# A conditioned decoder layer on one core: the first two modulations, with half of the row tiles of w_ada multiplied on TensorE

## The chip, the cores and the metric

One NeuronCore of a Trainium2 chip runs the whole layer in one launch. The metric is the device time of that launch in microseconds (us), as the median of several runs. A lower time is better. TensorE is called PE here (PEld is its weight load), VectorE DVE, ScalarE ACT, GpSimd POOL, and SyncE SP, which issues the transfers.

## What is computed

The reference is one layer of a decoder with adaptive normalization. What matters here is its beginning, for x of 1024 tokens by 1024 features and one condition vector c of 1024:

```python
c_act = jax.nn.silu(c)
mod = c_act @ w_ada[l] + b_ada[l]            # w_ada: 1024 x 9216
sh1, sc1, ga1, sh2, sc2, ga2, sh3, sc3, ga3 = jnp.split(mod, 9, axis=-1)
h = modulate(rms_norm(x, g_ffn1[l]), sh1, sc1)       # h * (1 + scale) + shift
x = x + 0.5 * ga1[:, None, :] * swiglu(h, w_gate1[l], w_up1[l], w_down1[l])
```

Then follow a mixer with two attention groups, a second SwiGLU with sh3, sc3 and ga3, and a last norm. The change touches sh1 and sc1, the first two of the nine modulations, and the squares of x for the first norm.

## The kernel before

x is held feature by feature: 8 tiles (NT) of 128 features by 1024 tokens in f_main. Large products are made of pairs of float32r operands, a high part (a cast, on ACT) and a low part (the rest, a subtraction on DVE for x and on POOL for weights), in three matmuls each; each engine runs its own program in order, and semaphores join them. The order is written out by hand.

The opening, up to the first product, goes so:

- SP (L741 to L750) issues x in four transfers of 1 MB, row tile 0 of the first gate and up weights (`pair_row`, 0.5 MB each), w_ada for the shift (j = 0) and the scale (j = 1) in four transfers of 1 MB each, two row tiles of 128 rows in each, and row tile 1 of gate and up.
- ACT squares the eight x tiles (L1491) into x_sq, splits two weights (`weight_high`, L1031), takes the root of the mean square of each half of the tokens (`std`, L997), copies DVE's sums out of PSUM (`ada_copy`, L1163), splits the other six weights of the first pair, and then goes in turns through `shifted` (L1008, x times nrm_a plus shift) and `x_high` (L1020, the cast).
- PE multiplies ones by each square tile (L2527, 8 tiles by two halves), then `mod_mm` (L2520) turns each of DVE's two sums into a modulation: 8 matmuls with a 128x128 float32 weight and a column of ones. The products of the first SwiGLU follow (`piece`, L2536 to L2538).
- DVE sums, for one modulation after the other, c_act times w_ada over the eight row tiles (`ada_start`: L1926 for the first, L1929 for the others) into PSUM, with the two reciprocals (L1831) between; then adds the bias (`mod`, L1934), makes nrm_a = (1 + scale) times gain (`shift_scale`, L1837), and the low parts of x (`x_low`, L1844).
- POOL splits off the low parts of the first two weights (`weight_low`, L1635), multiplies the first eight chunks of x by the reciprocal (`scaled_x`, L1630), does the other six weights and the other eight chunks.

A chunk is 128 features by 512 tokens; there are 16 of x. The first pair of weights has eight blocks (g = 0 to 7, PRELUDE), four of row tile 0 and four of row tile 1. PE goes through the first half of the tokens in two parts of four steps: a step multiplies one chunk with four blocks, twelve matmuls of 512 columns. Blocks 0 to 3 serve the first part, 4 to 7 the second. When POOL has done blocks 6 and 7, SP issues the next pair's loads (L650).

The other seven modulations are summed by DVE later, inside the first SwiGLU, and turned by the same `mod_mm`. The semaphore s_ada_used counts DVE's tiles, s_mod_mm PE's modulations, s_mods the finished ones.

Of the kernel before, what the change touches and what calls it, by code (L numbers as in the profile page):

```python
# [21 lines left out]
ALU = mybir.AluOpType  # L22
# [3 lines left out]
P = 128  # L26
D = 1024
T = 1024
NT = D // P
HALF = 512  # L30
NH = T // HALF
# [3 lines left out]
N_MOD = 9  # L35
# [125 lines left out]
GATE, UP = 0, 1  # L161
# [44 lines left out]
W_SUM_AT = {e: k + 1 for k, e in enumerate(W_SUM_ORDER)}  # L206
MOD_STEPS = [(j, part) for j in range(N_MOD) for part in ((0, 1) if j in (GA1, GA3) else (0,))]
MOD_AT = {e: k + 1 for k, e in enumerate(MOD_STEPS)}


# [66 lines left out]
def build(nc, aps, outs):  # L277
    ctx = ExitStack()
    with ctx:
# [3 lines left out]
        def sem(name):  # L283
            return ctx.enter_context(nc.semaphore(name))
# [75 lines left out]
        ps_mod0, ps_mod1 = ps[:, 4, 0:NT], ps[:, 5, 0:NT]  # L360
        ADA0 = 2 * NT
        ps_stat = ps[:, 6:8, :].rearrange("p a b -> p (a b)")
# [96 lines left out]
        s_ada = [sem(f"ada_in{r}") for r in range(8)]  # L459
        s_ada_used = sem("ada_used")  # L460
        s_mod_mm = sem("mod_mm")
        s_mods = sem("mods_done")
# [180 lines left out]
        def _(sp):  # L643
# [8 lines left out]
            def pair_row(f, b, row):  # L652
                sp.dma_start(pair_raw[b][:, row], w_pair[f][b][row]).then_inc(fsem[f][("row0", "raw")[row]][b], 16)
# [86 lines left out]
            for i in range(4):  # L740
                sp.dma_start(x[:, 2 * i:2 * i + 2, :], aps["xT"][2 * i:2 * i + 2].rearrange("n p t -> p n t")).then_inc(s_x[i], 16)  # L741
            for b in (GATE, UP):
                pair_row(0, b, 0)
            for j in range(2):
                for i in range(4):
                    sp.dma_start(ada_first[:, 16 * j + 2 * i:16 * j + 2 * i + 2, :],
                                 aps["w_ada"][2 * i * P:(2 * i + 2) * P, j * D:(j + 1) * D].rearrange("(r p) c -> p r c", p=P)).then_inc(s_ada[4 * j + i], 16)
            for b in (GATE, UP):
                pair_row(0, b, 1)
            gate_up_loads(0, 0)  # L750
# [226 lines left out]
        def _(act):  # L977
# [180 lines left out]

            def ada_copy(j):

                act.wait_ge(s_ada_used, NT * (j + 1))
                for h in range(NH):
                    act.copy(ada_sum[j][:, halves(h)], ada_acc[j][:, halves(h)]).then_inc(s_ada_sb, 1)  # L1163

            def x_added(base, s):
# [323 lines left out]
            for n in range(NT):  # L1489
                act.wait_ge(s_x[n // 2], 16)  # L1490
                act.activation(x_sq[n], x[:, n, :], ACT.Square).then_inc(nsem["sq"], 1)  # L1491
            for g in range(2):
                weight_high(0, g)
            std(0, 0)
            std(0, 1)
            ada_copy(0)
            ada_copy(1)
            for g in range(2, PRELUDE):
                weight_high(0, g)
            shifted(0, 0)  # L1500
            for i in range(4):
                shifted(0, i + 1)
                x_high(0, 1, i)
            first_pair(0, 0)
            gate_up(0)
# [85 lines left out]
        def _(pool):  # L1591
# [221 lines left out]
        def _(dve):  # L1813
# [96 lines left out]
            def ada(p, m):  # L1910

                dve.wait_ge(s_ada[m % 4], 16 * (1 + 2 * (p - 2) + m // 4 + 1))
                if m == 0:
                    if p > 2:
                        dve.wait_ge(s_ada_sb, 4 + p - 2)
                    dve.tensor_scalar(ps_stat, ada_raw[0], c_act[:, 0:1], None, ALU.mult).then_inc(s_ada_used, 1)
                else:
                    dve.wait_ge(s_ada_used, ADA0 + 8 * (p - 2) + m)
                    dve.scalar_tensor_tensor(ps_stat, ada_raw[m % 4], c_act[:, m:m + 1], ps_stat, ALU.mult, ALU.add).then_inc(s_ada_used, 1)

            def ada_start(j, m):

                acc, w = ada_acc[j], ada_first[:, 16 * j + m, :]
                dve.wait_ge(s_ada[4 * j + m // 2], 16)
                if m == 0:
                    dve.tensor_scalar(acc, w, c_act[:, 0:1], None, ALU.mult).then_inc(s_ada_used, 1)  # L1926
                else:
                    dve.wait_ge(s_ada_used, NT * j + m)
                    dve.scalar_tensor_tensor(acc, w, c_act[:, m:m + 1], acc, ALU.mult, ALU.add).then_inc(s_ada_used, 1)  # L1929

# [142 lines left out]
            dve.wait_ge(s_c, 1)  # L2073
            for m in range(4):
                ada_start(0, m)
            reciprocal(0, 0)
            for m in range(4, 6):
                ada_start(0, m)
            reciprocal(0, 1)
            for m in range(6, NT):  # L2080
                ada_start(0, m)
            for m in range(NT):
                ada_start(1, m)
# [417 lines left out]
        def _(pe):  # L2501
# [13 lines left out]

            def mod_mm(out, total, ready=None):
                for m in range(NT):
                    if ready is not None and m % 4 == 0:
                        pe.wait_ge(s_ada_sb, ready + m // 4 + 1)
# [4 lines left out]
            for n in range(NT):  # L2524
                pe.wait_ge(nsem["sq"], n + 1)
                for h in range(NH):
                    mm = pe.matmul(stat_of[0][h], ones_f[:], x_sq[n][:, halves(h)], start=n == 0, stop=n == NT - 1)  # L2527
                    if n == NT - 1:
                        mm.then_inc(nsem["mm"], 1)
            mod_mm(ps_mod0, ada_sum[0], 0)  # L2530
            mod_mm(ps_mod1, ada_sum[1], 2)
            pe.wait_ge(nsem["std"], 2)

# [24 lines left out]
            def gate_up(f, k):  # L2558
# [26 lines left out]
                for g in range(PRELUDE, N_PROD):  # L2585
# [10 lines left out]
                    if f == 0 and 2 <= p <= 8 and (b, q) == (UP, 4):  # L2596
                        pe.wait_ge(s_ada_sb, 4 + p - 1)
                        pe.wait_ge(s["sil"], z["sil"] + 4 * p + 3)
                        mod_mm(ps_mod, ada_sb)

            def down(f, norm):
# [3 lines left out]
                for e in DOWN:  # L2605
# [9 lines left out]
                    if t == 0:  # L2615
                        if n == 0 and f == 0:
                            pe.wait_ge(s_ada_sb, 4 + N_MOD - 2)
                        if n >= 2:
                            pe.wait_ge(s["sil" if n < 5 else "act"], z["sil" if n < 5 else "act"] + 4 * (PAIRS - 1) + (0, 0, 1, 4, 3, 1, 3, 4)[n])
# [361 lines left out]
```

## Time and profile before

| | |
|---|---|
| median of 3 runs | 2453.43 us (2452.48 to 2454.91) |
| profiled execution | 2450.02 us, of which the span is 2448.1 us |
| PE busy | 2316.3 us, 95% of the span |
| DVE, POOL, ACT busy | 1385.6, 1249.8, 1088.6 us |
| transfers | 314.98 MB, 129 GB/s in the mean |
| PE's first product | 58.47 us after the span's start |

The span runs from the first to the last instruction; the profiled execution is one run with its own time, and the rows further down are from it. In a timeline a row is: start, length (of several instructions in a row, from the first start to the last end), engine, line, operation, output<-input, shapes, count, and in brackets the idle time before it with what ended it. "issue" is time in which the engine waited for nothing that the profile shows. Matmul records are one or two per instruction: a float32 matmul leaves two.

### The profile page before, as it was taken

Reading aid. Unit: us, or ns where it says so; the run is one execution under the profiler, and the core shown is the slowest. Engines: PE = TensorE matmul, PEld = TensorE weight load, DVE = VectorE, ACT = ScalarE, POOL = GpSimd, SP = SyncE. Lnnn points to the kernel's source line nnn. Section 1 sums busy time; section 2 is a strip of 40 time slices with the busy share of each in tenths; the row PEclk is TensorE's granted clock in tenths of the full one; section 3 lists DMA queues with packets and bytes.
Section 4 is the critical chain, followed back from the end, with each engine's and each line's share of the span. In section 5 each row is a group of like instructions: output and inputs, shape, how many; then the busy total and the mean of one; then the engine's idle time right before and its main releaser. Section 6 shows DMA issues by size and latency. Waiting matters only on the chain. (4 is left out here: it accounts for less than half of the span.)

```text
span 2448.1 us, 30080 instructions
## 1 busy us (share of the span) xinstructions
PE 2316.3 (95%) x10920; PEld 1884.8 (77%) x10920; DVE 1385.6 (57%) x1664; ACT 1088.6 (44%) x2060; POOL 1249.8 (51%) x967
## 2 busy tenths in 40 slices
PE   4999999999999899999799999999789999999997
PEld 2788888888877777788677877777578888888885
DVE  5846555266557755742588888575463323225554
ACT  4533333323445443333688888423543333323332
POOL 3454444445564555444557545355745555435473
PEclk7999999999999999999899999999999999999998
DMA  6155544265451433343803046323212222245362
GB/s 254 59 185 176 189 174 160 75 227 168 151 168 48 142 120 128 143 170 129 248 14 88 18 110 173 105 93 130 94 53 85 83 82 94 73 169 175 116 188 88
DMA packets 128946, 314.98 MB, mean 129 GB/s; under 512 B 13408, under 2 KB 34016, under 8 KB 128800
## 3 DMA queue, kind: packets, MB, share of 16 engines
q1 hardware_dynamic: 127824, 310.76, 38.5%
q10 hardware_dynamic: 976, 2.29, 0.4%
q8 instruction: 88, 1.44, 0.2%
q14 instruction: 58, 0.48, 0.1%
HBM read 241.51 MB, written 69.34 MB: 127 GB/s over the span
## 5 line engine op out<-in xcount | busy, mean ns | idle before, releaser
L1635 POOL TENSOR_TENSOR r_z<-f_main,r_z 128x512 fp32r<-128x512 f32 x254 | 353.4, 1394 | 394.3 <-ACT r_z L1031 394.1
L2536 PE MATMUL ps<-r_main,r_z 128*128 128x512 f32 x1232 | 483.7, 393 | 21.4 <-issue 13.4
L2537 PE MATMUL ps<-r_main,r_z 128*128 128x512 f32 x1232 | 481.7, 391 | 0.0
L2538 PE MATMUL ps<-r_main,r_z 128*128 128x512 f32 x1232 | 481.4, 391 | 0.0
L1641 POOL TENSOR_TENSOR r_main<-f_main,r_main 128x1024 fp32r<-128x1024 f32 x88 | 217.0, 2469 | 221.3 <-ACT r_main L1072 221.3
L2536 PEld LDWEIGHTS ps<-r_main,r_z 128*128 128x128 f32 x1232 | 232.8, 189 | 71.3 <-issue 23.0
L2512 PE MATMUL ps<-r_main 128*128 128x512 f32 x688 | 269.0, 391 | 3.4 <-DVE r_main L1998 3.4
L2538 PEld LDWEIGHTS ps<-r_main,r_z 128*128 128x128 f32 x1232 | 232.8, 189 | 48.9
L2537 PEld LDWEIGHTS ps<-r_main,r_z 128*128 128x128 f32 x1232 | 232.9, 189 | 48.7 <-issue 0.2
L2514 PE MATMUL ps<-r_main 128*128 128x512 f32 x688 | 267.8, 389 | 0.0
L2513 PE MATMUL ps<-r_main 128*128 128x512 f32 x688 | 267.7, 389 | 0.0
L1031 ACT CAST r_z<-f_main 128x512 fp32r<-128x512 f32 x254 | 155.6, 618 | 235.6 <-PE ps L2538 216.3
L1668 POOL TENSOR_TENSOR r_z<-f_main,r_z 128x512 fp32r<-128x512 f32 x108 | 150.8, 1404 | 170.5 <-ACT r_z L1202 170.3
L1998 DVE TENSOR_TENSOR r_main<-f_main,r_main 128x512 fp32r<-128x512 f32 x66 | 140.4, 2129 | 138.8 <-ACT r_main L1074 138.6
L2705 PE MATMUL ps<-r_main,r_z 128*128 128x512 f32 x504 | 200.4, 398 | 12.8 <-DVE ps L2140 6.5
L2707 PE MATMUL ps<-r_main,r_z 128*128 128x512 f32 x504 | 198.1, 393 | 0.0
L2706 PE MATMUL ps<-r_main,r_z 128*128 128x512 f32 x504 | 198.0, 393 | 0.0
L1072 ACT CAST r_main<-f_main 128x1024 fp32r<-128x1024 f32 x88 | 92.5, 1051 | 215.6 <-PE ps L2514 123.4
L2339 DVE TENSOR_TENSOR r_main<-ps,r_main 128x512 fp32r<-128x512 f32 x244 | 151.8, 635 | 48.3 <-ACT r_main L1420 45.1
L2512 PEld LDWEIGHTS ps<-r_main 128*128 128x128 f32 x688 | 129.2, 188 | 32.3 <-POOL r_main L1641 4.9
L2513 PEld LDWEIGHTS ps<-r_main 128*128 128x128 f32 x688 | 129.2, 188 | 27.0 <-issue 0.5
L2514 PEld LDWEIGHTS ps<-r_main 128*128 128x128 f32 x688 | 129.1, 188 | 26.9
(309 smaller groups left out, 4626.8 us busy)
## 6 DMA issues: line engine op xcount, KB each, us to landing
f_main<-in_wd SPq DMA_DIRECT2D x88, 512.0 KB, 3.7
f_main<-in_w_ada SPq DMA_DIRECT2D x56, 512.0 KB, 5.1
act_d<-f_main SPq DMA_DIRECT2D x88, 256.0 KB, 2.0
f_main<-act_d SPq DMA_DIRECT2D x88, 256.0 KB, 3.8
f_main<-in_wg SPq DMA_DIRECT2D x20, 1024.0 KB, 5.0
f_main<-in_wu SPq DMA_DIRECT2D x20, 1024.0 KB, 5.1
f_main<-in_wmix SPq DMA_DIRECT2D x18, 1024.0 KB, 5.3
r_main<-qk_hi_d SPq DMA_DIRECT2D x40, 256.0 KB, 7.1
```

Of the source, the lines that this page charges most:

```text
L1031: act.copy(prod_hi_t[SLOTS[g]], source_of(g)).then_inc(s["wh"], 1)
L1635: pool.tensor_tensor(prod_lo_t[slot], source_of(g), prod_hi_t[slot].bitcast(F32), ALU.subtract).then_inc(s["wl"], 1)
L1641: pool.tensor_tensor(lo, down_w_raw[t % 2], hi.bitcast(F32), ALU.subtract).then_inc(s["dl"], 1)
L2512: pe.matmul(out, w, m, start=start, stop=False)
L2513: pe.matmul(out, w, ml, start=False, stop=False)
L2514: return pe.matmul(out, wl, m, start=False, stop=stop)
L2536: pe.matmul(out, wh, hi, start=start, stop=False, skip_group_check=True)
L2537: pe.matmul(out, wh, lo, start=False, stop=False, skip_group_check=True)
L2538: return pe.matmul(out, wl, hi, start=False, stop=stop, skip_group_check=True)
L2705: pe.matmul(out, wh, hi[:, k], start=q in (1, 7) and k == 0, stop=False, skip_group_check=True)
L2706: pe.matmul(out, wh, lo[:, k], start=False, stop=False, skip_group_check=True)
L2707: mm = pe.matmul(out, wl, hi[:, k], start=False, stop=k == 3, skip_group_check=True)
```

## The change

It concerns the opening alone.

- **Order of the modulations.** The scale (SC1) comes first in the transfers, in DVE's and in PE's program, the shift (SH1) second.
- **Who multiplies w_ada.** DVE keeps row tiles 0, 2, 4, 6 of the scale and 0, 2, 4 of the shift; the last step of each writes the sum into SBUF at once, so ACT's copies fall away. PE takes the other nine row tiles: each is eight matmuls with the 128x128 block of w_ada as weight and one column of c_act, accumulated in PSUM on top of the bias, which two matmuls with the identity put there first. DVE's sum is added with ones as before. DVE then only copies the modulation out.
- **Transfers.** Both row tiles of the gate and up weights are loaded after w_ada.
- **Squares.** DVE adds the squares of x in pairs, in place, and PE multiplies ones by four tiles instead of eight.
- **ACT and POOL.** Both begin the weights after the norm's part. ACT splits blocks 0 and 1, then 2 and 3 after the first chunk of x, then 4 to 7 after the fourth; POOL scales ten chunks of x, splits blocks 0 to 3, then 4 to 7 with a chunk of x between them.

```diff
-MOD_STEPS = [(j, part) for j in range(N_MOD) for part in ((0, 1) if j in (GA1, GA3) else (0,))]
+MOD_ORDER = (SC1, SH1, *range(2, N_MOD))
+MOD_STEPS = [(j, part) for j in MOD_ORDER for part in ((0, 1) if j in (GA1, GA3) else (0,))]
...
+ADA_DVE = {SC1: (0, 2, 4, 6), SH1: (0, 2, 4)}
+ADA0 = len(ADA_DVE[SC1]) + len(ADA_DVE[SH1])
...
-            for b in (GATE, UP):
-                pair_row(0, b, 0)
-            for j in range(2):
+            for j in (SC1, SH1):
                 for i in range(4):
                     sp.dma_start(ada_first[:, 16 * j + 2 * i:16 * j + 2 * i + 2, :],
                                  aps["w_ada"][2 * i * P:(2 * i + 2) * P, j * D:(j + 1) * D].rearrange("(r p) c -> p r c", p=P)).then_inc(s_ada[4 * j + i], 16)
-            for b in (GATE, UP):
-                pair_row(0, b, 1)
+            for row in range(2):
+                for b in (GATE, UP):
+                    pair_row(0, b, row)
...
-            for g in range(2):
-                weight_high(0, g)
             std(0, 0)
             std(0, 1)
-            ada_copy(0)
-            ada_copy(1)
-            for g in range(2, PRELUDE):
+            for g in range(2):
                 weight_high(0, g)
             shifted(0, 0)
             for i in range(4):
                 shifted(0, i + 1)
                 x_high(0, 1, i)
+                if i == 0:
+                    for g in range(2, 4):
+                        weight_high(0, g)
+            for g in range(4, PRELUDE):
+                weight_high(0, g)
...
-            for g in range(2):
+            for m in range(NT + 2):
+                scaled_x(0, m)
+            for g in range(4):
                 weight_low(0, g)
-            for m in range(NT):
-                scaled_x(0, m)
-            for g in range(2, PRELUDE):
+            for g in range(4, PRELUDE):
                 weight_low(0, g)
-            for m in range(NT, 16):
+                scaled_x(0, NT + g - 2)
+            for m in range(14, 16):
                 scaled_x(0, m)
...
             def ada_start(j, m):
 
-                acc, w = ada_acc[j], ada_first[:, 16 * j + m, :]
+                w, ms = ada_first[:, 16 * j + m, :], ADA_DVE[j]
+                at = ms.index(m)
                 dve.wait_ge(s_ada[4 * j + m // 2], 16)
...
+                if at == 0:
+                    dve.tensor_scalar(ada_acc[j], w, c_act[:, m:m + 1], None, ALU.mult).then_inc(s_ada_used, 1)
+                else:
+                    dve.wait_ge(s_ada_used, at + (0 if j == SC1 else len(ADA_DVE[SC1])))
+                    out = ada_sum[j] if m == ms[-1] else ada_acc[j]
+                    dve.scalar_tensor_tensor(out, w, c_act[:, m:m + 1], ada_acc[j], ALU.mult, ALU.add).then_inc(s_ada_used, 1)
+
+            def squares_paired(i):
+
+                dve.wait_ge(nsem["sq"], 2 * i + 2)
+                dve.tensor_tensor(x_sq[2 * i], x_sq[2 * i], x_sq[2 * i + 1], ALU.add).then_inc(s_x_sq, 1)
...
-            mod(SH1, ps_mod0)
-            mod(SC1, ps_mod1)
+            ada_start(SH1, 2)
+            ada_start(SH1, 4)
+            mod_start(SC1, ps_mod0)
             shift_scale(0)
+            mod_start(SH1, ps_mod1)
...
+            def ada_mm(out, j, k):
+                pe.wait_ge(s_ada[4 * j + k // 2], 16)
+                for m in range(NT):
+                    mm = pe.matmul(out[:, m:m + 1], ada_first[:, 16 * j + k, m * P:(m + 1) * P], c_act[:, k:k + 1], start=False,
+                                   stop=(j, k) == (SH1, NT - 1), skip_group_check=True)
+                return mm
...
+            for i in range(4):
+                stat_first(i)
+            pe.wait_ge(s_c, 1)
+            pe.wait_ge(q_["const"], 3)
+            for j, out in ((SC1, ps_mod0), (SH1, ps_mod1)):
+                pe.matmul(out, ident_f[:], b_ada[:, j, :], start=True, stop=False, skip_group_check=True)
+            for k in (1, 3, 5, 7):
+                ada_mm(ps_mod0, SC1, k)
+            ada_total(ps_mod0, SC1).then_inc(s_mod_mm, 1)
+            for k in (1, 3, 5):
+                ada_mm(ps_mod1, SH1, k)
+            ada_total(ps_mod1, SH1)
+            ada_mm(ps_mod1, SH1, 6)
+            ada_mm(ps_mod1, SH1, 7).then_inc(s_mod_mm, 1)
```

`ada_total` waits for DVE's last tile of that modulation and multiplies its sum by ones (eight matmuls); `mod_start` waits for PE and copies the modulation; `stat_first` waits for a pair of squares and multiplies it in two halves.

How this stands in the programs of the engines. On PE, at the start, before (the second row is the squares, the third `mod_mm` for both modulations, the fourth the first product):

```order
L2500 UNCONDITIONAL_BRANCH
L2527 MATMUL ps<-f_r,ones_f 128x512 x16
L2520 MATMUL ps<-ones_f,f_r 128x1 x16
L2536 MATMUL ps<-r_main,r_z 128x512
L2537 MATMUL ps<-r_main,r_z 128x512
```

and changed:

```order
L2538 MATMUL ps<-f_r,ones_f 128x512 x8
L2561 MATMUL ps<-b_ada_sb,ident_f 128x8 x2
L2545 MATMUL ps<-c_act,f_r 128x1 x32
L2552 MATMUL ps<-ones_f,f_r 128x1 x8
L2545 MATMUL ps<-c_act,f_r 128x1 x24
L2552 MATMUL ps<-ones_f,f_r 128x1 x8
L2545 MATMUL ps<-c_act,f_r 128x1 x16
L2574 MATMUL ps<-r_main,r_z 128x512
```

The squares are halved, and 88 one-column matmuls and two of eight columns stand where 16 of one column stood.

On POOL, from the first weight or chunk of x to the last of the opening (L1635 and L1634 are `weight_low`, L1630 and L1629 `scaled_x`), before:

```order
L1635 TENSOR_TENSOR r_z<-f_main,r_z 128x512 x2
L1630 TENSOR_TENSOR f_main<-f_main 128x512 x8
L1635 TENSOR_TENSOR r_z<-f_main,r_z 128x512 x5
L1635 TENSOR_TENSOR r_main<-f_main,r_main 128x512
L1630 TENSOR_TENSOR f_main<-f_main 128x512 x8
```

and changed:

```order
L1629 TENSOR_TENSOR f_main<-f_main 128x512 x10
L1634 TENSOR_TENSOR r_z<-f_main,r_z 128x512 x5
L1629 TENSOR_TENSOR f_main<-f_main 128x512
L1634 TENSOR_TENSOR r_z<-f_main,r_z 128x512
L1629 TENSOR_TENSOR f_main<-f_main 128x512
L1634 TENSOR_TENSOR r_z<-f_main,r_z 128x512
L1629 TENSOR_TENSOR f_main<-f_main 128x512
L1634 TENSOR_TENSOR r_main<-f_main,r_main 128x512
L1629 TENSOR_TENSOR f_main<-f_main 128x512 x3
```

Ten chunks of x come before the first weight, and three stand between the last four weights.

On DVE, up to the factor nrm_a (L1837) and the low parts of x (L1844), the difference:

```order
-L1926 TENSOR_SCALAR ps<-f_r,c_act 128x1024
-L1929 SCALAR_TENSOR_TENSOR ps<-f_r,c_act,ps 128x1024 x3
+L1936 TENSOR_TENSOR f_r<-f_r 128x1024 x4
+L1927 TENSOR_SCALAR ps<-f_r,c_act 128x1024
+L1931 SCALAR_TENSOR_TENSOR ps<-f_r,c_act,ps 128x1024
 L1831 RECIPROCAL f_main<-f_main 128x512
```

Four additions of squares come first, and two tiles instead of four stand before the first reciprocal.

## Rows read from the trace of the kernel before

**Rows 1.** The page's part 1: busy us, share of the span, instructions
```profile
PE 2316.3 (95%) x10920; PEld 1884.8 (77%) x10920; DVE 1385.6 (57%) x1664; ACT 1088.6 (44%) x2060; POOL 1249.8 (51%) x967
```

**Rows 2.** Busy by window: each engine's us and count, PE clock, DMA share, GB/s
```profile
0.00:58.47 58.47, 23.10 (x64) 13.80 (x65) 28.77 (x22) 21.78 (x31) 20.34 (x26) 0.77 0.66 255
58.47:103.00 44.53, 44.53 (x189) 36.72 (x190) 39.87 (x44) 26.70 (x45) 21.18 (x14) 0.96 0.17 60
```

**Rows 3.** Timeline of DVE (start, length, line, operation, count, idle before)
```profile
22.00 1.29 DVE L1926 TENSOR_SCALAR ps<-f_r,c_act 128x1024 f32<-128x1024 f32 x1 [22.00 <-DMA f_r<-in_w_ada]
...
40.31 9.64 DVE L1929 SCALAR_TENSOR_TENSOR ps<-f_r,c_act,ps 128x1024 f32<-128x1024 f32 x7
...
54.23 0.17 DVE L1934 TENSOR_TENSOR mods<-ps,b_ada_sb 128x8 f32<-128x8 f32 x1 [4.22 <-PE ps L2520]
54.43 0.96 DVE L1837 SCALAR_TENSOR_TENSOR nrm_a<-mods,gains_sb 128x8 f32<-128x8 f32 x1
...
77.21 0.68 DVE L1851 TENSOR_TENSOR f_main<-f_main 128x512 f32<-128x512 f32 x1
...
89.51 0.68 DVE L1875 TENSOR_TENSOR s<-f_main 128x512 f32<-128x512 f32 x1
...
92.98 3.62 DVE L1844 TENSOR_TENSOR r_main<-f_main,r_main 128x512 fp32r<-128x512 f32 x4 [2.19 <-ACT r_main L1020]
```

**Rows 4.** Timeline of ACT, 16 to 57 us
```profile
16.80 2.00 ACT L1491 ACTIVATE f_r<-f_main 128x1024 f32<-128x1024 f32 x2 [0.56 <-DMA f_main<-in_xT]
...
50.94 2.70 ACT L1031 CAST r_z<-f_main 128x512 fp32r<-128x512 f32 x5
...
55.43 1.52 ACT L1008 ACTIVATE f_main<-f_main,mods,nrm_a 128x512 f32<-128x512 f32 x2 [1.27 <-DVE nrm_a L1837]
```

**Rows 5.** Timeline of PE's matmuls and of its weight loads (PEld)
```profile
10.35 15.94 PE L2527 MATMUL ps<-f_r,ones_f 128*128 128x512 f32 x32 [10.35 <-ACT f_r L1491]
...
50.62 3.49 PEld L2520 LDWEIGHTS ps<-ones_f,f_r 128*128 128x128 f32 x16 [7.44 <-ACT f_r L1163]
...
179.03 1.98 PEld L2520 LDWEIGHTS ps<-ones_f,f_main 128*128 128x128 f32 x16
180.93 0.19 PEld L2536 LDWEIGHTS ps<-r_main,r_z 128*128 128x128 f32 x1
```

**Rows 6.** Windows (PE, its clock, DMA share, GB/s) and timeline of PE
```profile
31.00:32.00 1.00, 0.00 (x0) 0.70 1.04 414
39.00:44.00 5.00, 3.58 (x16) 0.50 0.53 211
58.47:62.00 3.53, 3.53 (x8) 0.50 0.81 289
836.00:837.00 1.00, 1.00 (x9) 0.97 0.00 0
915.00:915.50 0.50, 0.50 (x3) 0.95 0.86 352
...
835.85 2.88 PE L2736 MATMUL ps<-r_f 128*128 128x256 f32 x16 [3.97 <-issue]
...
914.49 0.47 PE L2705 MATMUL ps<-r_main,r_z 128*128 128x512 f32 x1 [1.81 <-DVE ps L2140]
```

**Rows 7.** Timeline of POOL and of SP's queue
```profile
30.80 9.82 POOL L1630 TENSOR_TENSOR f_main<-f_main 128x512 f32<-128x512 f32 x8 [8.92 <-DVE f_main L1831]
...
59.47 13.65 POOL L1630 TENSOR_TENSOR f_main<-f_main 128x512 f32<-128x512 f32 x8
...
57.85 0.38 SPq L650 DMA_DIRECT2D f_main<-in_wg  x1
59.54 0.38 SPq L650 DMA_DIRECT2D f_main<-in_wu  x1
```

**Rows 8.** Window of the last transfers; the next pair's loads (us to landing)
```profile
41.00:42.00 1.00, 1.00 (x6) 0.50 0.58 229
...
f_main<-in_wu SPq DMA_DIRECT2D x1, 1024.0 KB, 8.0
```

More of the change, by code:

```diff
@@ L360, in build @@
         ps_mod0, ps_mod1 = ps[:, 4, 0:NT], ps[:, 5, 0:NT]
-        ADA0 = 2 * NT
         ps_stat = ps[:, 6:8, :].rearrange("p a b -> p (a b)")
@@ L460, in build @@
         s_ada_used = sem("ada_used")
+        s_x_sq = sem("x_squares_paired")
         s_mod_mm = sem("mod_mm")
@@ L1157, in final @@
                 act.activation(x[:, n, halves(h)], nrm_u[u % 2], ACT.Copy, scale=gains[:, 3, n:n + 1]).then_inc(s_fin_a, 1)
[L1159 to L1163, printed above, removed]
             def x_added(base, s):
@@ L1914, in ada @@
                     if p > 2:
-                        dve.wait_ge(s_ada_sb, 4 + p - 2)
+                        dve.wait_ge(s_ada_sb, p - 2)
                     dve.tensor_scalar(ps_stat, ada_raw[0], c_act[:, 0:1], None, ALU.mult).then_inc(s_ada_used, 1)
@@ L1921, in ada_start, with mod_start @@
             def ada_start(j, m):
-                acc, w = ada_acc[j], ada_first[:, 16 * j + m, :]
+                w, ms = ada_first[:, 16 * j + m, :], ADA_DVE[j]
+                at = ms.index(m)
                 dve.wait_ge(s_ada[4 * j + m // 2], 16)
-                if m == 0:
-                    dve.tensor_scalar(acc, w, c_act[:, 0:1], None, ALU.mult).then_inc(s_ada_used, 1)
-                else:
-                    dve.wait_ge(s_ada_used, NT * j + m)
-                    dve.scalar_tensor_tensor(acc, w, c_act[:, m:m + 1], acc, ALU.mult, ALU.add).then_inc(s_ada_used, 1)
+                if at == 0:
+                    dve.tensor_scalar(ada_acc[j], w, c_act[:, m:m + 1], None, ALU.mult).then_inc(s_ada_used, 1)
+                else:
+                    dve.wait_ge(s_ada_used, at + (0 if j == SC1 else len(ADA_DVE[SC1])))
[4 more added lines that the diff above has]
+                dve.tensor_tensor(x_sq[2 * i], x_sq[2 * i], x_sq[2 * i + 1], ALU.add).then_inc(s_x_sq, 1)
+            def mod_start(j, out):
+                dve.wait_ge(s_mod_mm, MOD_ORDER.index(j) + 1)
+                dve.tensor_copy(mods[:, j, :], out).then_inc(s_mods, 1)
             def mod(j, out):
@@ L2073, in _ @@
             dve.wait_ge(s_c, 1)
-            for m in range(4):
-                ada_start(0, m)
+            for i in range(4):
+                squares_paired(i)
+            ada_start(SC1, 0)
+            ada_start(SC1, 2)
             reciprocal(0, 0)
-            for m in range(4, 6):
-                ada_start(0, m)
+            ada_start(SC1, 4)
+            ada_start(SC1, 6)
+            ada_start(SH1, 0)
             reciprocal(0, 1)
[L2080 to L2083, printed above, removed]
-            mod(SH1, ps_mod0)
-            mod(SC1, ps_mod1)
+            ada_start(SH1, 2)
+            ada_start(SH1, 4)
+            mod_start(SC1, ps_mod0)
             shift_scale(0)
+            mod_start(SH1, ps_mod1)
             for i in range(4):
@@ L2514, in product3, with mod_mm @@
                 return pe.matmul(out, wl, m, start=False, stop=stop)
-            def mod_mm(out, total, ready=None):
+            def mod_mm(out, total):
                 for m in range(NT):
-                    if ready is not None and m % 4 == 0:
-                        pe.wait_ge(s_ada_sb, ready + m // 4 + 1)
                     mm = pe.matmul(out[:, m:m + 1], total[:, m * P:(m + 1) * P], ones_f[:, 0:1], start=True, stop=True)
@@ L2523, in _, with stat_first, ada_total @@
             pe.wait_ge(s_const, 3)
-            for n in range(NT):
-                pe.wait_ge(nsem["sq"], n + 1)
+            def stat_first(i):
+                pe.wait_ge(s_x_sq, i + 1)
                 for h in range(NH):
-                    mm = pe.matmul(stat_of[0][h], ones_f[:], x_sq[n][:, halves(h)], start=n == 0, stop=n == NT - 1)
-                    if n == NT - 1:
+                    mm = pe.matmul(stat_of[0][h], ones_f[:], x_sq[2 * i][:, halves(h)], start=i == 0, stop=i == 3)
+                    if i == 3:
                         mm.then_inc(nsem["mm"], 1)
-            mod_mm(ps_mod0, ada_sum[0], 0)
-            mod_mm(ps_mod1, ada_sum[1], 2)
+            def ada_mm(out, j, k):
[4 more added lines that the diff above has]
+                return mm
+            def ada_total(out, j):
+                pe.wait_ge(s_ada_used, len(ADA_DVE[SC1]) + (len(ADA_DVE[SH1]) if j == SH1 else 0))
+                for m in range(NT):
+                    mm = pe.matmul(out[:, m:m + 1], ada_sum[j][:, m * P:(m + 1) * P], ones_f[:, 0:1], start=False,
+                                   stop=j == SC1, skip_group_check=True)
+                return mm
+            for i in range(4):
+                stat_first(i)
[11 more added lines that the diff above has]
+            ada_mm(ps_mod1, SH1, 7).then_inc(s_mod_mm, 1)
             pe.wait_ge(nsem["std"], 2)
@@ L2596, in gate_up @@
                     if f == 0 and 2 <= p <= 8 and (b, q) == (UP, 4):
-                        pe.wait_ge(s_ada_sb, 4 + p - 1)
+                        pe.wait_ge(s_ada_sb, p - 1)
                         pe.wait_ge(s["sil"], z["sil"] + 4 * p + 3)
@@ L2616, in down @@
                         if n == 0 and f == 0:
-                            pe.wait_ge(s_ada_sb, 4 + N_MOD - 2)
+                            pe.wait_ge(s_ada_sb, N_MOD - 2)
                         if n >= 2:
```

## The prediction, made before the changed kernel was run

> **What bounds the kernel now.** The page first [rows 1]: PE is busy for 95% of the span, so only PE's idle stretches are open. Two windows show the largest of them [rows 2]: until 58.47 us PE works 23.10 of 58.47 us, and after it it does not stop for 44.5 us. The end of this opening is what the change is about. Later on PE sets the pace itself, so I take it that every microsecond by which the first product comes earlier or later goes through to the end.
>
> Who keeps PE waiting stands in the timeline by engine. DVE starts the 16 row tiles of the two modulations at 22.00 us, when their first transfer has landed, and works without a gap through 16 tiles of about 1.37 us and two reciprocals until 49.9 us [rows 3]. Then ACT copies the sum, PE multiplies it by ones until 54.2 us, DVE makes the modulation and the factor nrm_a [rows 3], ACT scales and casts x from 55.43 us [rows 4], and PE begins at 58.47 us. So DVE ends the wait; the transfers don't: they are through at about 41.6 us [rows 8].
>
> **The change, part by part.** Times are from the span's start.
>
> *Squares.* ACT's last pair of squares ends at 18.80 us [rows 4]. DVE now adds each pair; the nearest row has 0.68 us for half its columns [rows 3], so I take 1.25 us each, the last done at 20.1. PE had 32 records of the squares from 10.35 to 26.29 us [rows 5]; 16 are left. They start with the first pair at about 12.4 us. Four took 3.4 us at half clock and take 1.7 us at full clock, and the full clock comes after 3.6 to 4.1 us of such work, so PE is through with three pairs when the fourth is ready, and done at 21.8 us instead of 26.3.
>
> *Transfers.* The whole opening moves the same bytes at about 410 GB/s [rows 6], 2.56 us for 1 MB. The first w_ada transfer landed at 22.00 us behind 1 MB of weights, so now at 19.4, the others every 2.56 us: the scale's last at 27.1, the shift's last at 37.4, the four weight rows from 38.6 to 42.5 us.
>
> *DVE.* 7 tiles instead of 16, in SBUF or PSUM as before: 20.1 to about 29.4 us for the scale (one reciprocal inside), 36.9 us for the shift. It no longer ends the wait. ACT's copies ahead of PE go.
>
> *PE.* This is the new bound. It gets eleven groups of 8 one-column matmuls with a fresh 128x128 float32 weight each (nine of w_ada, two of DVE's sums), against two groups before, and two seeds with the bias. A group is what the 16 records of L2520 are: 3.50 us at half clock (3.49 in PE's weight loads) and 1.90 us at full clock, between the weight loads of 179.03 and 180.93 us [rows 5]. The two prices give 11 x 1.90 + 0.5 = 21.4 us or 11 x 3.50 + 0.9 = 39.4 us. Everything hangs on the clock.
>
> *The clock.* The records show two levels, 1.0 (2.4 GHz) and 0.5 (1.2 GHz). It fell near 31.4 us, 5.1 us after the squares; near 836.9, 5.1 us after the last wide product though PE was at work again from 835.85; near 915.45, 2.8 us after PE stopped, though it had been back for a microsecond [rows 6]. So work at the moment of the fall doesn't hold it: it takes a history of it. Whether thin matmuls are such work, no row settles. At half clock 3.5 us of them did not raise it, twice [rows 5, 6], where 3.6 us of 512-column products from 58.47 did; at full clock 1.9 us of them among wide products kept it. I take them as no work for the clock: a one-column matmul sends one column in the time of a weight load, and the two bursts that failed were as long as the wide one that didn't. Then the clock falls 3 to 5 us after the squares, say 4: at 25.8 us. From 21.8 to 25.8 PE does the seeds and 1.85 groups; 9.15 are left at 3.50: 32.0 us. The shift is ready at 57.8 us, where it was at 54.2: **+3.6 us**. Each microsecond by which the clock falls sooner or later moves this by 0.85.
>
> *The tail.* nrm_a needs the scale alone, which is done first, at about 37 us. From DVE's shift to ACT's first scaling goes the 0.96 us of L1837 [rows 3]: **-1.0 us**. ACT's and POOL's first weights are ready long before (the rows land until 42.5).
>
> *The interleaved order of ACT and POOL.* Before, all eight weight pairs were split ahead of x, under the wait. Now four are split after the first scaled chunk, and POOL places a scaling of x between them. After PE's start, counted from it: ACT casts weights 4 to 7 at 4 to 6 us (0.54 us each [rows 4]); POOL then runs L1635 and L1630 in turn, 1.23 us each with DVE in PSUM and 1.71 with DVE's splits beside it [rows 7], so the last, weight 7, is there at 14.5 to 16 us. PE needs it after 57 of its products: 12 or so at half clock and 45 at 0.2273 us, 15.3 us. I take **+0.5 us**, between 0 and 2. The next pair's transfers wait for weights 6 and 7: they left at 57.85 and 59.54 us [rows 7] and will leave at about 73 and 77, land up to 8 us later [rows 8], and are first read by DVE near 92 (89.51 before [rows 3]): hidden. DVE's low parts of x end some 4 us later relative to PE; idle time such as the 2.19 us before 92.98 [rows 3] takes most of it up.
>
> Sum: 3.6 - 1.0 + 0.5 = **+3.1 us** on the profiled execution's 2450.0 us. The median of the timed runs is 2453.4, 3.4 us above that execution, and the change is laid on the median: **2456.5 us**. Differences up to 0.2% (4.9 us) are about what a measurement of this kernel can't tell from none.
>
> On the weight load a page speaks against my price. The weight loads of a group take 3.49 us at half clock and 1.90 at full [rows 5], so their cost goes with the clock. The Trainium skill (TensorE: Matmul & The Clock Gate, LDWEIGHTS) puts a load at its columns over 1.2, in ns, with no word of the clock: an estimate from it is 16 x 107 ns = 1.7 us for a group at either level, the shift ready at 41.1 us, and about 2440 us in all. At half clock the rows contradict it by a factor of two, and my sum follows them.
>
> **Rivals.**
>
> *The clock stays up* (0.28). PE is never idle between the squares and the shift, only its columns are few. Then the shift is ready at 21.8 + 21.4 = 43.2 us; no transfer (37.4) and no DVE sum (36.9) comes later. 43.2 - 54.2 = -11.0, the tail -1.0, and about +0.8 for POOL's order: -11.2, **2442.2 us**. For it: the burst of 179.03 us in which the clock held. Against: that burst lasted 1.9 us only, wide products on both sides. The Trainium skill names this mechanism (same page, What's actually happening): the gate goes by how busy PE has been recently, which read plainly keeps it open here. No row decides it.
>
> *The clock is down at once, and POOL's order shows* (0.24, the side of a loss). The fall of 915.45 us came 2.8 us after work ended; with gaps between the pairs of squares the full clock may hardly hold into the thin groups, or never be reached before them. From 21.8 us, 39.4 us at half clock: 61.2, +7.0 against before, the tail -1.0, POOL at 1.71 us throughout +1 to +2: +7 to +8, **2460.9 us**. It decides from the point where less than 2 us of the thin work runs at full clock, or where weight 7 comes over 2 us late.
>
> *It doesn't matter* would need the PE chain hidden; nothing else is left at 57 us to hide it (DVE 36.9, transfers 42.5), so I give that no chance of its own.
>
> **How the numbers follow.** The forecast, a small loss at the half clock, has 0.48; its own range is 2453.5 to 2458.5. The range that holds 8 in 10 must reach into the first rival and nearly through the second: 2440 to 2461. Faster by over 0.2% is the first rival, 0.28; within 0.2% the forecast, less its upper edge, 0.46; slower the second and that edge, 0.26.
>
> **What would show it.** The eleven thin groups from 22 us: their mean length and the granted clock beside them (3.50 us each from about 26 us on: right; 1.9 throughout: the first rival). The scale's modulation near 37 us, the shift's near 58. PE's first product near 61.2 us. POOL's weight 7 at 14.5 to 16 us after that, with a stop of PE under 2 us. nrm_a long before the shift. I am wrong if the first product comes before 50 us, or if PE's stops after it grow by more than 3 us.

## The result, and the profile after

The change takes 2458.05 us in the median (2452.56 to 2462.49, 19 runs), the kernel before 2453.03 us beside it (2449.9 to 2455.67, 19 runs): a ratio of **1.0018, 95% interval 1.0012 to 1.0024**. The forecast was 2456.5 us, a small loss. The profiled execution took 2458.24 us with a span of 2456.3; the one of before lies 3 us under its own median, so the two profiled executions differ by more (8.2 us) than the medians (5.0).

The timeline of PE in the opening, against [rows 5] (start, length, engine, line, operation, output<-input, count, idle before):

```profile
12.90 9.49 PE L2538 MATMUL ps<-f_r,ones_f 128*128 128x512 f32 x16 [12.90 <-DVE f_r L1936]
22.23 0.51 PE L2561 MATMUL ps<-b_ada_sb,ident_f 128*128 128x8 f32 x4
22.59 9.61 PE L2545 MATMUL ps<-c_act,f_r 128*128 128x1 f32 x64
32.06 3.55 PE L2552 MATMUL ps<-ones_f,f_r 128*128 128x1 f32 x16
35.47 10.38 PE L2545 MATMUL ps<-c_act,f_r 128*128 128x1 f32 x48
45.71 3.55 PE L2552 MATMUL ps<-ones_f,f_r 128*128 128x1 f32 x16
49.12 6.96 PE L2545 MATMUL ps<-c_act,f_r 128*128 128x1 f32 x32
59.23 0.76 PE L2574 MATMUL ps<-r_main,r_z 128*128 128x512 f32 x1 [3.15 <-issue]
```

PE works without a stop from 22.23 to 56.08 us, and its first product comes 0.76 us later than the 58.47 of [rows 2]. The four groups in the first L2545 row take 9.61 us; from 32.06 us on, each group starts 3.41 us after the one before. The windows of the same kernel (length, busy us and count of PE, PEld, DVE, ACT, POOL, then PE's clock, DMA share, GB/s) say why:

```profile
27.00:28.00 1.00, 1.00 (x7) 1.00 (x7) 0.90 (x2) 0.00 (x0) 1.00 (x1) 0.60 1.01 406
27.60:56.10 28.50, 28.49 (x134) 28.40 (x134) 9.17 (x8) 1.24 (x2) 14.09 (x12) 0.50 0.51 203
119.60:123.10 3.50, 3.50 (x10) 2.68 (x10) 0.00 (x0) 0.44 (x1) 2.31 (x2) 0.55 0.01 2
```

The clock falls at 27.2 us (0.60 over the window 27 to 28 is the full clock for a fifth of it), 4.8 us after the squares, and stays at its lower level (1.2 GHz) for the whole chain while PE is busy for 28.49 of 28.50 us. DVE's timeline shows who ends the wait now, where [rows 3] had DVE busy until 49.9 us:

```profile
35.97 1.28 DVE L1931 SCALAR_TENSOR_TENSOR f_r<-f_r,c_act,ps 128x1024 f32<-128x1024 f32 x1 [0.41 <-DMA f_r<-in_w_ada]
37.17 0.16 DVE L1941 COPY mods<-ps 128x8 f32<-128x8 f32 x1
37.36 0.60 DVE L1837 SCALAR_TENSOR_TENSOR nrm_a<-mods,gains_sb 128x8 f32<-128x8 f32 x1
56.13 0.17 DVE L1941 COPY mods<-ps 128x8 f32<-128x8 f32 x1 [18.17 <-PE ps L2545]
```

DVE has its sums at 37.25 us and waits 18.17 us for PE. Behind the first product, POOL's split of the last of the first eight weight blocks (weight 7), which was done at 59.5 us before, when the second transfer of [rows 7] left, and the end of a stop of PE further on:

```profile
72.60 1.74 POOL L1634 TENSOR_TENSOR r_main<-f_main,r_main 128x512 fp32r<-128x512 f32 x1
...
119.02 0.47 PE L2574 MATMUL ps<-r_main,r_z 128*128 128x512 f32 x1 [2.53 <-issue]
```

POOL has weight 7 at 74.34 us, 15.1 us after the first product, and PE doesn't stop for it. The stop that ends at 119.02 us was there before too, 1.72 us long and ending at 116.57; it is 0.8 us longer now.

To size these I count matmuls from the last one backwards and compare the start of the same one in two traces; "displacement" below is that difference against the profiled execution of before. For the change it is +0.8 us at the first product, +1.6 once the full clock is back (64.7 us, 5.5 us after the first product; before it took 3.6 us), +4.0 at 124 us and the same until 400 us. The stop gives 0.8 of the last step; the rest is the half clock after it (third window row), which this execution alone has. After 780 us the displacement wanders, up to 8.7 us, at clock falls whose instants differ from one execution to the next (near 800, 840, 1210, 1810, 2200 us). It wanders in all the traces below, upwards by 1.4 to 2.9 us between 1790 and 1840 us in every one: the profiled execution of before was the luckier one there.

### The profile page after: what moved, and what is told of

It reads as the page before. It is cut to its first block and busy times, and to the rows that moved or that the text cites. A ratio compares the mean times of both kernels' runs of the same rounds, so it can differ in the third digit from the quotient of the medians.

```text
span 2456.3 us, 30327 instructions
## 1 busy us (share of the span) xinstructions
PE 2340.0 (95%) x11052; PEld 1911.7 (78%) x11052; DVE 1378.6 (56%) x1659; ACT 1088.1 (44%) x2056; POOL 1252.3 (51%) x967
## 5 line engine op out<-in xcount | busy, mean ns | idle before, releaser
L1634 POOL TENSOR_TENSOR r_z<-f_main,r_z 128x512 fp32r<-128x512 f32 x254 | 355.9, 1403 | 382.2 <-ACT r_z L1035 382.2
```

Of the source, the lines that this page charges most:

```text
L1634: pool.tensor_tensor(prod_lo_t[slot], source_of(g), prod_hi_t[slot].bitcast(F32), ALU.subtract).then_inc(s["wl"], 1)
```

## The experiments

The theory that stood first, A: the clock falls under thin multiplications (a fresh 128x128 weight for one column) although PE is busy without a stop. Beside it stand the questions of what the new order of ACT and POOL costs, and what PE's part costs beside the rest of the change. The letters B to E and P in the expectations name the rivals; each is described where it stands.

**Wide products between the thin ones.** In front of each of the eleven groups, two float32 products of 512 columns whose result nobody reads.

```diff
+            def wide():
+                for _ in range(2):
+                    pe.matmul(stat_of[0][0], ones_f[:], x_sq[0][:, halves(0)], start=True, stop=True)
```

> Two wide float32 matmuls (ones by a square tile, 512 columns, 0.86 us each at full clock) stand ahead of each of the eleven thin groups, 18.9 us of added work. Theory A (thin matmuls are no work for the clock, wide ones are): the granted clock stays at 1.0 through the opening, a group takes 1.9 us, the last ends near 63 us and the first product starts near 66 us; the launch takes some 6 us more than the changed kernel, 2464. Rival B (the clock falls about 5 us after the squares whatever follows, as it fell in all openings so far): the fills take 1.7 us each and a group 3.4, the first product starts near 100 us, the launch takes over 2490 us.

Measured: 2459.76 us (one run). PE's timeline and the window over both modulations:

```profile
24.14 1.84 PE L2552 MATMUL ps<-c_act,f_r 128*128 128x1 f32 x16
25.84 1.96 PE L2544 MATMUL ps<-f_r,ones_f 128*128 128x512 f32 x4
59.17 1.84 PE L2552 MATMUL ps<-c_act,f_r 128*128 128x1 f32 x16
64.15 0.77 PE L2582 MATMUL ps<-r_main,r_z 128*128 128x512 f32 x1 [3.14 <-issue]
...
20.00:64.00 44.00, 40.86 (x228) 29.30 (x228) 16.33 (x14) 5.31 (x9) 14.90 (x13) 1.00 0.51 201
```

The clock stays at 1.00 for 44 us, and the same group takes 1.70 us from its start to the next instruction's, half of 3.41. (The first two records of a group start 0.02 us apart behind the wide products. In the change, where a group follows a group, the full clock gives 1.79 us: the first three start at 22.59, 24.38 and 26.16 us.) The eleven groups cost 18.7 us so, against 33.5 us in the change; the fillers take more than that saves, and the first product comes 4.9 us later. It is a single run, so its time says little; the trace decides. Same thin work, PE busy without a stop in both (here 38.60 of 38.60 us from 22.40 to 61.00), another clock: theory A holds, and rival B, a fall some 5 us after the squares whatever follows, is out. The Trainium skill (TensorE: Matmul & The Clock Gate, What's actually happening) lets the clock follow how busy PE has been; if "busy" is read as the profile counts it, these two traces don't agree with it, since PE is 100% busy in both and only one keeps the full clock.

**DVE keeps all sixteen tiles**, the rest of the change stays (the lists of DVE's and PE's steps follow the constant).

```diff
-ADA_DVE = {SC1: (0, 2, 4, 6), SH1: (0, 2, 4)}
+ADA_DVE = {SC1: (0, 1, 2, 3, 4, 5, 6, 7), SH1: (0, 1, 2, 3, 4, 5, 6, 7)}
```

> All 16 row tiles back on DVE; the pairs of squares, the order of the modulations, the transfers and ACT's and POOL's order stay as changed. Theory A (the loss is PE's nine groups at half clock, the other parts gain): DVE ends near 48 us, PE's sum near 51.5, first product near 54.5 us, 4 us earlier than before: 2449 to 2450 us. Rival C (the loss lies in the other parts: weights loaded last, interleaved order): no faster than before, 2453 or more.

Measured: 2449.8 us (11 runs), ratio 0.9993 (0.9984 to 1.0002). First product 55.10 us, 3.4 us before that of the kernel before (4 were expected); the displacement at 200 us is -2.0 us, since the two places of the order, described below, take 1.2 us back. The gain is in the trace; in the times the interval still reaches 1. PE's clock while nothing at all runs on it between the squares and the first sum:

```profile
24.00:25.00 1.00, 0.00 (x0) 0.00 (x0) 1.00 (x1) 0.00 (x0) 0.00 (x0) 0.93 1.04 418
25.00:26.00 1.00, 0.00 (x0) 0.00 (x0) 1.00 (x1) 0.00 (x0) 0.00 (x0) 0.50 1.05 418
...
48.38 3.58 PE L2561 MATMUL ps<-ones_f,f_r 128*128 128x1 f32 x16 [7.36 <-DVE f_r L1931]
55.10 0.76 PE L2581 MATMUL ps<-r_main,r_z 128*128 128x512 f32 x1 [3.15 <-issue]
```

Here PE is idle from 23.0 us and the clock falls at 24.9 us (at 27.0 us in the same division with the old order, below); with the thin groups in that place it fell between 24.4 and 27.2 us. Within this spread the thin groups held the clock no longer than idleness did, which is theory A seen from the other side.

**The change in the old order of ACT and POOL**: all eight weights split ahead of x.

```diff
-            for g in range(2):
+            for g in range(PRELUDE):
                 weight_high(0, g)
...
-            for g in range(4):
-                weight_low(0, g)
-            for g in range(4, PRELUDE):
+            for g in range(PRELUDE):
                 weight_low(0, g)
-                scaled_x(0, NT + g - 2)
```

> The change, but ACT and POOL split all eight weights of the first pair ahead of the first scaled chunk. Theory A: first product near 59.2 us as changed; the stop of PE near 117 us goes back from 2.5 to 1.7 us and with it the clock's fall there, so 1 to 2 us faster than the change, 2456 to 2457. Rival C (the interleaved order is the loss): 5 us faster than the change, 2453 or less.

Measured: 2453.36 us (11 runs), ratio 1.0002 (0.9994 to 1.0011). Beside the 2458.05 us of the first measurement that looked like an order worth over 4 us, as rival C had it, but the profile spoke for less: first product at 61.37 us, displacement +3.0 us. Theory D below is that cost of 4 us; its rivals are E (no more than the 0.8 us of the stop) and P (0.8 to 1.3 us, what the stops show).

**A split by cost**: DVE eleven tiles, PE five.

```diff
+ADA_DVE = {SC1: (0, 2, 4, 5, 6), SH1: (2, 3, 4, 5, 6, 7)}
...
+            for k in (1, 3, 7):
+                ada_mm(ps_mod0, SC1, k)
...
+            for k in (0, 1):
+                ada_mm(ps_mod1, SH1, k)
```

> DVE takes 11 row tiles (scale 0, 2, 4, 5, 6, shift 2 to 7), PE five (scale 1, 3, 7, shift 0, 1). Theory A: DVE ends near 41.7 us, PE by then has its groups behind it, adds DVE's sum in 3.4 us, first product near 48.5 us, 10 us before the kernel before: 2443 to 2445 us. Rival C: the loss stays, 2453 or more.

Measured: 2444.77 us (5 runs), ratio 0.9963 (0.9949 to 0.9976). First product 48.59 us, displacement -8.8 us: faster than both kernels, with the rest of the change in place, so rival C, a loss in that rest, is out.

The change again, and both of these divisions in the old order of ACT and POOL:

> The change unaltered, beside the others on one chip. Theory D (the interleaved order of ACT and POOL costs about 4 us, by a longer stop of PE near 117 us and what the clock does there): 0.18% over before again, about 4 us over the change with the old order, 2456 to 2458 us when before has 2452. Rival E (the earlier comparison across sets of runs misled, the order costs no more than the 0.8 us of the stop): within 2 us of the change with the old order.

> All 16 row tiles on DVE and the eight weights split ahead of x. First product near 55.1 us as with the interleaved order. Theory D: 2 to 4 us faster than the same kernel with the interleaved order, so 2447 us. Rival E: the same within 1 us, 2449 to 2450 us.

> DVE 11 row tiles, PE five, and the eight weights split ahead of x. First product near 48.7 us, or up to 1 us later, since the last weight lands at 42.5 us and eight casts follow. Theory D: 2441 to 2443 us, 2 to 4 us faster than with the interleaved order. Rival E: 2444 to 2445 us.

Measured: the change 1.0012 (1.0003 to 1.0021); DVE alone, old order, 0.9987 (0.9978 to 0.9996); eleven tiles, old order, 2443.22 us, 0.9964 (0.9952 to 0.9977). In the last one PE and DVE end together:

```profile
34.09 6.96 PE L2541 MATMUL ps<-c_act,f_r 128*128 128x1 f32 x32
41.94 3.58 PE L2548 MATMUL ps<-ones_f,f_r 128*128 128x1 f32 x16 [0.89 <-DVE f_r L1923]
49.97 0.77 PE L2568 MATMUL ps<-r_main,r_z 128*128 128x512 f32 x1 [4.45 <-issue]
```

PE waits 0.89 us for DVE's last tile, where in the change DVE waited 18.17 us for PE.

**The wide form**: the column of c_act is the weight (one column) and w_ada moves in 512 columns; the modulation comes out as a row, which DVE copies and PE turns with eight small matmuls. Old order.

```diff
+                for h in range(NH):
+                    mm = pe.matmul(row_ps[j][h], c_act[:, k:k + 1], ada_first[:, 16 * j + k, halves(h)], start=first, stop=(j, k) == (SH1, 7),
+                                   skip_group_check=True)
```

> PE keeps its nine row tiles but with the column of c_act as the weight and w_ada as the moving operand: 22 wide float32 matmuls of 512 columns (0.86 us each at full clock) give each modulation as one row, DVE copies it, eight matmuls turn it into columns; old order of ACT and POOL. Theory A: the clock stays at 1.0 until the first product, 22.3 us + 18.9 + 1.8 for turning the scale = 43 us, copy and turning 1.5 to 2.5, first product at 47.5 to 49 us, 2441 to 2443 us. Rival B (the clock falls about 5 us after the squares all the same): rows at 1.7 us a matmul, the first product after 60 us, over 2453 us.

Measured: 2452.04 us, ratio 0.9995 (0.9986 to 1.0003), far from what was expected. PE's timeline and a window:

```profile
31.46 1.88 PE L2548 MATMUL ps<-f_r,c_act 128*1 128x512 f32 x4
38.02 3.41 PE L2564 MATMUL ps<-ones_f,f_r 1*128 1x1 f32 x16 [4.67 <-DVE f_r L1937]
41.35 5.42 PE L2548 MATMUL ps<-f_r,c_act 128*1 128x512 f32 x8
57.95 0.77 PE L2586 MATMUL ps<-r_main,r_z 128*128 128x512 f32 x1 [4.16 <-issue]
...
38.00:45.00 7.00, 6.99 (x21) 3.91 (x22) 1.61 (x3) 3.74 (x7) 6.49 (x6) 0.52 0.55 219
```

I had put the turning of the scale in front of the shift's rows, and DVE makes the copy for it only after its shift tiles: PE stands for 4.67 us, the clock falls, and the next seven microseconds run at half of it. So the run tested a wait, not the form. With the turning behind the shift's rows:

```diff
             ada_row(SH1, 1, True)
-            turned(SC1, 1)
             ada_row(SH1, 3)
             ada_row(SH1, 5)
             row_total(SH1)
+            turned(SC1, 1)
```

> The wide form again (the column of c_act as weight, w_ada moving in 512 columns), with one thing mended: in the run before it PE stood still for 4.67 us from 33.35 us, in front of the turning of the scale's row, because DVE makes the copy of that row only after its shift tiles (37.3 us); the clock fell at 38.6 us, and the turning and the next four products ran at half clock. Now the turning stands behind the shift's rows 1, 3, 5 and DVE's shift sum, so PE waits in pieces of at most 2 us. Theory A (the change is at half clock because thin multiplications are no work for the clock, and it is the half clock alone that costs): the clock stays at 1.0 through the two modulations, the last turning ends near 48 us, the first product comes at 51 to 53 us instead of 57.95, and the time is 5 to 7 us under the one before it: ratio 0.9967 to 0.9977. Rival: the pieces of waiting add up and the clock falls all the same near 38 us; then the first product comes at 55 to 57 us, ratio 0.9985 to 0.9995.

Measured: 2444.3 us (2441.83 to 2448.32, 9 runs), **ratio 0.9975 (0.9965 to 0.9984)**, as theory A had it (the first product half a microsecond before the range expected):

```profile
40.99 3.59 PE L2548 MATMUL ps<-f_r,c_act 128*1 128x512 f32 x8
44.52 1.94 PE L2564 MATMUL ps<-ones_f,f_r 1*128 1x1 f32 x16
50.53 0.76 PE L2586 MATMUL ps<-r_main,r_z 128*128 128x512 f32 x1 [4.07 <-issue]
...
12.00:46.50 34.50, 32.59 (x92) 10.64 (x92) 23.61 (x20) 11.93 (x16) 18.85 (x16) 1.00 0.88 353
```

Row tiles are divided as in the change, the clock stays up until 47.8 us, when PE has nothing left to do, and the first product comes 8.7 us earlier than in the change. (The clock column reads 1.00 from 12 us, but the first squares still start 0.85 us apart and only from 17.3 us on 0.43 us apart: before about 17 us the column can't be relied on. The stretch that counts runs from there.) A tile of w_ada costs 1.75 us this way at full clock (four records, start to start), about what a thin group does there (1.70); the gain is the clock.

**The order once more**, measured side by side:

> The change once more, beside the old order in the same session, to size what the new order of transfers and casts costs. Reading so far of the profiled executions, against the kernel before at the same product 200 us into the span: the change +4.03 and +3.15 us, the change in the old order +3.03 us with TensorE's clock fallen 3 us earlier (24.3 us instead of 27.5). Theory P (the order costs what the two stops near 75 and 117 us show): 0 to 0.5 us at the weight row plus 0.8 us at the second stop, so this kernel is 0.8 to 1.3 us (0.03 to 0.05%) above the old order, with the second stop at 2.5 us here. Theory D (the order costs about 4 us): 0.15% above it. Ratio to the kernel before expected 1.0010 to 1.0018.

> The change's sums in the order of transfers and casts of before, once more. Theory P: second stop 1.72 us, no stop at the weight row, ratio to the kernel before 1.0005 to 1.0012, 0.03 to 0.05% under the change of the same session. Theory D: ratio 1.0000 to 1.0002, 0.15% under it. Beside that: the clock of TensorE falls at an instant that both theories leave free, 24 to 28 us; every microsecond that it falls later moves the first product about one microsecond forward (the group of 16 thin multiplications takes 1.7 us at full clock and 3.41 us at half).

Measured: 1.0013 (1.0004 to 1.0022) and 1.0013 (1.0003 to 1.0023). The 4 us of the earlier comparison are not there, and the other two pairs (0.9993 and 0.9987, 0.9963 and 0.9964) don't show them either: theory D is out. The times can't tell an order worth 1 us from none. What it does cost stands in every pair of traces: 0 to 0.8 us near weight 7, and more at PE's stop some 60 us after the first product. First DVE and POOL in the old order (the second run of it), then in the change:

```profile
106.99 2.69 DVE L1836 TENSOR_TENSOR r_main<-f_main,r_main 128x512 fp32r<-128x512 f32 x4 [1.89 <-ACT r_main L1024]
109.61 1.77 DVE L1877 TENSOR_TENSOR f_main<-f_main 128x512 f32<-128x512 f32 x1
...
109.12 1.72 POOL L1629 TENSOR_TENSOR r_z<-f_main,r_z 128x512 fp32r<-128x512 f32 x1 [1.79 <-ACT r_z L1035]
```

```profile
105.30 4.60 DVE L1844 TENSOR_TENSOR r_main<-f_main,r_main 128x512 fp32r<-128x512 f32 x4 [2.51 <-ACT r_main L1024]
109.83 0.68 DVE L1885 TENSOR_TENSOR f_main<-f_main 128x512 f32<-128x512 f32 x1
...
101.19 5.26 POOL L1634 TENSOR_TENSOR r_z<-f_main,r_z 128x512 fp32r<-128x512 f32 x3 [3.76 <-ACT r_z L1035]
107.43 1.32 POOL L1634 TENSOR_TENSOR r_z<-f_main,r_z 128x512 fp32r<-128x512 f32 x1 [0.98 <-ACT r_z L1035]
```

A DVE subtraction of one chunk takes 0.68 us alone and 1.77 us when POOL's operation overlaps it. In the old order one of these five subtractions meets POOL, together 4.4 us; in the new one POOL is at work until 106.45 and again from 107.43 us, and the five take 5.2. Counted from the start of the first of them, PE's last product before the stop ends after 11.2 us in both, and its next one begins after 12.9 us in the old order and 13.7 in the new. PE's stop behind them is 1.71 or 1.72 us in before and in all six traces of the old order, and 2.21 to 2.54 us in all six of the new. That POOL's overlap is the cause is read from these rows and was not tried by itself. The Trainium skill (SBUF — State Buffer, Who interferes with whom) says that a DVE instruction with two SBUF inputs contends with a GpSimd instruction that reads SBUF, over a pair of ports that the two share. These subtractions are such instructions on both sides, and the 0.68 and 1.77 us fit it.

All together (all times in us; the fall of the clock after the squares; the displacement at 200 us into the span):

| kernel | clock falls | first product | stop near 108-123 | displacement | ratio (95%) |
|---|---|---|---|---|---|
| the change | 27.2 | 59.23 | 2.53 | +4.0 | 1.0018 (1.0012 to 1.0024) |
| the same, again | 25.9 | 60.31 | 2.53 | +3.2 | 1.0012 (1.0003 to 1.0021) |
| the same, third | 24.5 | 61.47 | 2.54 | +4.4 | 1.0013 (1.0004 to 1.0022) |
| old order | 24.4 | 61.37 | 1.72 | +3.0 | 1.0002 (0.9994 to 1.0011) |
| old order, again | 24.9 | 61.35 | 1.72 | +3.3 | 1.0013 (1.0003 to 1.0023) |
| wide products between (one run) | 64.0 | 64.15 | 2.21 | +6.7 | none |
| DVE all | 24.9 | 55.10 | 2.52 | -2.0 | 0.9993 (0.9984 to 1.0002) |
| DVE all, old order | 27.0 | 55.40 | 1.72 | -2.1 | 0.9987 (0.9978 to 0.9996) |
| DVE eleven | 24.8 | 48.59 | 2.21 | -8.8 | 0.9963 (0.9949 to 0.9976) |
| DVE eleven, old order | 26.8 | 49.97 | 1.72 | -8.3 | 0.9964 (0.9952 to 0.9977) |
| wide, with the wait | 38.2 | 57.95 | 1.71 | -0.3 | 0.9995 (0.9986 to 1.0003) |
| wide, mended | 47.8 | 50.53 | 1.72 | -7.7 | 0.9975 (0.9965 to 0.9984) |

## Why the prediction was right, point by point

*The opening.* The forecast of a half clock under the thin groups was right, and with it the new bound: PE, not DVE (29.26 and 37.25 us against 29.4 and 36.9 foretold) and not the transfers. Squares done at 22.4 us (21.8), shift ready at 56.1 (57.8), first product at 59.2 (61.2). Of the two microseconds 1.2 are the instant of the fall: "say 4" us after the squares gave 25.8, and it was 27.2 (1.4 us x 0.85). In the five executions of these thin groups it was 24.4 to 27.2; the two later falls have their first product at 59.2 and 60.3, the three early ones at 61.4 to 61.5, and the mean of the five is 60.7. The rest is the group's price, less some 0.5 us for a later start: from start to start 3.41 us at half clock, not 3.50, since the length of a row of 16 includes the tail of its last one, and 1.79 at full, not 1.90.

*The tail.* Right: from the shift to the first product 3.10 us (56.13 to 59.23) where it was 4.24, so -1.1 against -1.0.

*The interleaved order.* Weight 7 was there 15.1 us after the first product (14.5 to 16 foretold), with a stop of 0, 0.49 and 0.1 us in three executions (0.5 foretold, between 0 and 2). (Wide products follow each other by 0.2267 us in the trace of before, not 0.2273; the 15.3 us stay.) The next pair's loads left 11.7 and 15.1 us after the first product, hidden as foretold. The step that failed is "idle time ... takes most of it up": DVE's work on x does not only come later, it meets POOL differently, and PE's stop near 117 us grows by 0.8 us. Of the displacement, 0.8, 1.6 and 1.2 us arise at these two places in the three executions, where +0.5 was taken; the half clock behind the stop in the profiled one is not counted.

*The sum.* 3.1 us foretold; the displacement of the three executions is +3.2 to +4.4, and their ratios give +2.9 to +4.4 us. The forecast of 2456.5 us stands between the three medians of the change, 2455.3, 2455.6 and 2458.1. The way and the bound were right, but that the size agrees so well is in part luck. The terms up to the first product were +2.6 us, and the profiled execution had +0.8 there (the other two +1.8 and +3.0). Weight 7 took 0, 0.8 and 0.4 us, for which +0.5 stood. Then came what no term had: the clock's return, beside that of before, +0.9 us in the profiled one (-0.2 and +0.2 in the others), 0.8 us more of the stop near 117 us in each, and the half clock behind it, +1.6 us, in that one alone.

*Which part costs what.* DVE with all tiles stands at -2.0 us and the change at +3.2 to +4.4: nine tiles on PE **cost 5 to 6.5 us**, and the rest of the change (the pairs of squares, the transfers, nrm_a ahead, no copies on ACT) **gains 2**. This is read at 200 us from single traces; in the medians the change with DVE's sixteen tiles is 1.9 us (new order) and 3.2 us (old order) under before, and only the second is clear of the noise. The prediction priced the sum and not this division.

*The rivals.* The clock staying up was refuted for the change as it stands. Where it did stay up, with wide products in the place of thin ones, the displacement was -7.7 us and the median 7.4 us under before, where -11.2 had been worked out (another form, which needs a copy and a turning for each modulation). The third case (2460.9) was to begin where less than 2 us of the thin work runs at full clock; the earliest falls left just 2.0 us of it, with the first product at 61.4 us, so it stayed at that edge. The estimate of 2440 us came from the Trainium skill (TensorE: Matmul & The Clock Gate, LDWEIGHTS), whose figure gives 1.7 us for 16 loads of 128 columns. The traces agree with it at full clock (1.70 us behind wide products, 1.79 in a chain) and contradict it at half clock (3.41 us), as the rows had said.

## What to carry to other kernels

In every trace here in which thin groups followed one another, they kept PE 100% busy and the clock still fell, after which a group cost 3.41 us instead of 1.79; so price such a chain at the half clock, or turn the operands round so that the wide one moves and the one-column one is the weight. Divide work between two engines by what a piece costs on each (here 1.4 us on DVE against 3.41 us on PE at half clock): the division that ended both together was worth 0.5% over the change's nearly equal halves. And where two executions of the same kernel differ by several microseconds through the instants at which the clock falls, compare the displacement of the same instruction right behind the change, and only then the ends.

## What was not expected of the hardware

- With two products of 512 columns before each thin group (16 records) the clock stood at 1.00 for 44 us; without them it was at 0.50 from 2.2 to 4.8 us after the last wide product on, much as where PE was idle instead (2.2 and 4.4 us).
- A stop of 4.67 us was enough for the clock to fall 4.9 us after the last product (33.3 to 38.2 us), when PE had just been back for 0.2 us; stops of 0.2 to 0.4 us in the mended version did nothing.
- The clock's return after the first product took 5.5 us in one execution and 3.2 us in another of the same kernel. What sets these instants is left open; in the five executions of the change's thin groups the displacement once the clock is back lies between +1.6 and +3.3 us.
